# Reading the page numbers of the sample attention eight at a time into registers

## The chip, the cores and the metric

The kernel runs on one core of a Trainium2 chip. Five engines work side by side, each with a sequencer of its own that takes instructions in order: TensorE (PE in the profile, PEld for its weight loads), VectorE (DVE), ScalarE (ACT), GpSimd (POOL) and SyncE (SP, which only issues transfers and waits). They meet through semaphores. The metric is the device time of one execution in microseconds; lower is better.

## The reference, cut to what matters

One inference step of a two-layer decoder: layer 0 is multi-head latent attention, layer 1 an RWKV-7 time mix, each with a feed-forward block behind it. Beside a prompt of 528 tokens there are eight samples of four new tokens each. A sample attends to 4096 past positions, which lie in a paged cache: 32 pages of 128 positions, each page 256 latent columns and 64 rope columns. Which physical page holds which logical page is read from a table:

```
page_table   (DEC_BATCH, PAST_LEN // PAGE_SIZE) int32      logical page -> physical page
...
    s = jnp.einsum('bhtr,bsr->bhts', q_lat, c) + jnp.einsum('bhtp,bsp->bhts', q_rope, kr)
    s = s.astype(jnp.float32) * SOFTMAX_SCALE
    s = jnp.where(k_pos[None, :] <= q_pos[:, None], s, jnp.finfo(jnp.float32).min)
    p = jax.nn.softmax(s, axis=-1).astype(c.dtype)
    return jnp.einsum('bhts,bsr->bthr', p, c)
```

For a sample, `c` and `kr` are its 32 pages followed by its four new rows.

## The kernel before

The kernel is written engine by engine: a block holds one instruction stream for each engine, in a fixed order, and semaphores tie the streams together. The page table lies in SBUF as `ptab`, one row of 256 numbers.

**Where pages go.** There are two sets of page buffers, `u` = 0 and 1; sample b uses set b % 2. A set's 32 pages are in four groups of eight (`GP = 8`), with semaphores of their own: `page_full` and `ropes_full` say that a group has landed, `page_used` that PE has read it for the last time.

**Who issues the transfers.** `load_pages` is called by three engines, each for its part of the same groups. In the sample attention SP brings the latents of the pages whose number is not 3 modulo 4 (six of eight in a group), POOL the ropes of the same pages, and ACT both parts of the other two pages. For each page it loads one number from `ptab` into a register (line 564), checks that it lies in the pool, and issues one transfer (line 567, latent) or two (lines 567 and 571). Samples 0 and 1 are loaded by SP and POOL alone, during the prompt attention, with table positions known when the program is built. For samples 2 to 7 the loads stand in loops (`Fori`) over k, two samples to a turn.

**The sample attention.** PE turns the keys of four pages at a time (g = 0 to 7, and the new rows as g = 8) and scores them; ACT copies what PE turned out of PSUM (line 961 the rope part, line 965 the latents); PE mixes with the weights of the sample before in between (line 906), which sets that sample's pages free. So the copies of a sample are nine steps on ACT's stream. ACT's own page loads stand in this stream: behind the copies of steps 5, 6, 7 and 8 come the loads of groups 0, 1, 2 and 3 of the next sample that uses the freed set:

```
if g >= 5 and load is not None:
    load_pages(act, *load, [3], [3], [g - 5])
```

While six of the eight samples are copied, a set is refilled for a later sample; for the first and the last sample copied there is nothing to load beside the copies. ACT's stream also holds the exponents of the sample before (line 977), behind the copies of step 1.

Of the kernel before, what the change touches and what calls it, by code (L numbers as in the profile page):

```python
# [17 lines left out]
ALU = mybir.AluOpType  # L18
ACT = mybir.ActivationFunctionType
AX = mybir.AxisListType.X  # L20

P = 128
D = 1024
# [13 lines left out]
PAGE, PAGES = 128, 32  # L37
# [104 lines left out]
def program(nc, w, o):  # L142

    ctx = ExitStack()
    with ctx:
# [31 lines left out]
        ptab = sb("ptab", [1, DB * PAGES], I32)  # L177
# [108 lines left out]
        xtok, _ = carve(0, 5, D)  # L286
        vrow, _ = carve(5 * D, 2, P)
# [66 lines left out]
        at = 0  # L354
        q, at = carve(at, 3, H, T)
        q_end = at
        kT, at = carve(at, 3, T)
        ctok, at = carve(at, 5, KL + ROPE)
        after_keys = at
        z, at = carve(at, ZC, T)  # L360
        qn, at = carve(at, 2, T)
        ukT, at = carve(at, 2, KL)
        rt, at = carve(at, 2, T)
# [171 lines left out]
        even_lat, at = carve(after_keys, PAGES, KL)  # L535
        even_rope, at = carve(at, PAGES // 2, 2 * ROPE)
        cnew, at = carve(at, DB, KL + ROPE)
        LB = wb.all.shape[1] // KL
        RA = (PAGES - LB) * KL
        ropes = [wa.all[:, a:a + 2 * ROPE] for a in range(RA, wa.all.shape[1] - 2 * ROPE + 1, 2 * ROPE)][:PAGES // 2]  # L540
        while len(ropes) < PAGES // 2:
            more, at = carve(at, 2 * ROPE)
# [5 lines left out]
        GP = 8  # L548
# [3 lines left out]
        ptab_in, cnew_in = sem("ptab_in"), sem("cnew_in")  # L552
        n_pool = w["cache_latent"].shape[1]

        def load_pages(eng, k, u, latents=(), ropes=(), groups=range(PAGES // GP)):


            for g in groups:
                if not isinstance(k, int):
                    eng.wait_ge(page_used[u][g], k)  # L560
                for p in range(g * GP, (g + 1) * GP):
                    if p % 4 not in {*latents, *ropes}:
                        continue
                    page = eng.value_load(ptab[0:1, bass.ds(k * (2 * PAGES) + (u * PAGES + p), 1)], min_val=0,
                                          max_val=n_pool - 1)
                    if p % 4 in latents:
                        eng.dma_start(lat_of[u][p], w["cache_latent"][0, page]).then_inc(page_full[u][g], 16)
                    if p % 4 in ropes:

                        full = (page_full if p % 4 == 3 else ropes_full)[u][g]  # L570
                        eng.dma_start(rope_of[u][p // 2][:, p % 2 * ROPE:(p % 2 + 1) * ROPE],  # L571
                                      w["cache_krope"][0, page]).then_inc(full, 16)
# [139 lines left out]
        with nc.Block(no_gpsimd_drain=True) as block:  # L712
            @block.sync
            def _(sp):
                sp.dma_start(ptab[:], w["page_table"].rearrange("b n -> (b n)").rearrange("(a n) -> a n", a=1)).then_inc(ptab_in, 16)
                for b in range(DB):
                    sp.dma_start(cnew[0:DS, b], ctok[TAIL + b * DS:TAIL + (b + 1) * DS, 4]).then_inc(cnew_in, 16)
                sp.wait_ge(ptab_in, 16)
                load_pages(sp, 0, 0, range(4), [3])
                load_pages(sp, 0, 1, range(4), [3])  # L720

            @block.gpsimd
            def _(pool):
                pool.wait_ge(ptab_in, 16)
                load_pages(pool, 0, 0, ropes=range(3))
                load_pages(pool, 0, 1, ropes=range(3))

            @block.tensor
            def _(pe):
                scores(pe, 0, 0, 0)  # L730

                def step(i, u, g, gn, an):
                    if gn is not None:
                        scores(pe, i + 1, 1 - u, gn)
                    turn_and_mix(pe, i, u, g)
                over_tiles(pe, step)

            @block.scalar
            def _(act):
                exponents(act, 0, 0, 0)  # L740

                def step(i, u, g, gn, an):
                    if gn is not None:
                        keep_below(act, i + 1, 1 - u, gn)
                    keep_turned(act, i, u, g)
                    if gn is not None:
                        exponents(act, i + 1, 1 - u, gn)
                    keep_mixed(act, i, u, g)
                over_tiles(act, step)

            @block.vector
            def _(dve):
                stage(dve, 0, 0)
                stage(dve, 1, 1)
                mask_and_max(dve, 0, 0, 0, 0)
                weigh(dve, 0, 0, 0)

                def step(i, u, g, gn, an):
                    if not isinstance(i, int) or i + 2 < NT:
                        stage(dve, i + 2, u)  # L760
                    if gn is not None:
                        mask_and_max(dve, i + 1, 1 - u, gn, an)
                        weigh(dve, i + 1, 1 - u, gn)
                over_tiles(dve, step)
# [21 lines left out]
        kts, _ = carve(q_end, 2, 10, P)  # L786
        omix, _ = carve(q_end + 20 * P, RC, P)
        maxes, _ = carve(q_end + 22 * P, 4)
        sums, _ = carve(q_end + 22 * P + 4, 4)
        shift, _ = carve(q_end + 22 * P + 8, 1)  # L790
        of_q, _ = carve(q_end + 22 * P + 16, NQ)
        recip, _ = carve(q_end + 22 * P + 16 + NQ, NQ)
# [23 lines left out]
        with nc.Block(no_gpsimd_drain=True) as block:  # L816
            @block.sync
            def _(sp):
                with sp.Fori(1, DB // 2) as k:
                    for u in range(2):  # L820
                        load_pages(sp, k, u, range(3))

                for g in range(PAGES // GP):
                    sp.wait_ge(page_used[0][g], DB // 2)
                sp.dma_start(wuv, w["attn_w_uv"][0].rearrange("(c p) h n -> p c (h n)", p=P)).then_inc(wuv_in, 16)

            @block.gpsimd
            def _(pool):
                with pool.Fori(1, DB // 2) as k:
                    for u in range(2):  # L830
                        load_pages(pool, k, u, ropes=range(3))

            @block.tensor
            def _(pe):
# [116 lines left out]
            @block.scalar  # L951
            def _(act):
                def copies(b, before=None, load=None):

                    for g in range(NG + 1):
                        keys = turned_keys(g)
                        act.wait_ge(gscored, b * (NG + 1) + (g - 1 if 2 <= g < NG else 0) + FREE)
                        act.wait_ge(rope_turned, b * (NG + 1) + (g + 1))
                        r = slice(8, 10) if g < NG else slice(2, 3)
                        n = 2 if g < NG else 1  # L960
                        nc.scalar.copy(keys[:, r], ps[:, ROT, 0:n * P].rearrange("p (c n) -> p c n", n=P)).then_inc(rope_copied, 1)
                        for half in range(2 if g < NG else 1):
                            n = 4 if g < NG else 2
                            act.wait_ge(lat_turned, b * LATS + (g * 2 + half + 1))
                            nc.scalar.copy(keys[:, half * 4:half * 4 + n],
                                           ps[:, LAT[half], 0:n * P].rearrange("p (c n) -> p c n", n=P)).then_inc(lat_copied, 1)
                        if g == 1 and before is not None:
                            exponents(before)
                        if g >= 5 and load is not None:
                            load_pages(act, *load, [3], [3], [g - 5])  # L970

                def exponents(b):
                    act.wait_ge(shifted, b + 1 + FREE)
                    ge(act, p_turned, b * 2)
                    ge(act, sums_in, b)
                    for half in range(2):
                        nc.scalar.activation(probs_b[:, half * 4:half * 4 + 4], ps[:, SCORES + half].rearrange("p (g n) -> p g n", n=P),
                                             ACT.Exp, bias=shift, scale=SCALE, accum_out=sums[:, half:half + 1]).then_inc(exped_b, 1)
                    nc.scalar.activation(p_new[0:NQ], s_new[0:NQ], ACT.Exp, bias=shift[0:NQ], scale=SCALE,
                                         accum_out=sums[0:NQ, 2:3]).then_inc(exped_b, 1)  # L980

                copies(0)

                def step(k, u, b, last):
                    if last < 2:
                        copies(b + 1, b, None if last else (k + 1, u))
                    else:
                        exponents(b)
                over_batches(act, step)
# [1384 lines left out]
```

## Time and profile before

| what | value |
|---|---|
| three runs, lowest / median / highest | 2320.49 / 2325.57 / 2333.77 us |
| the profiled execution: its time | 2321.38 us |
| its span, first to last instruction | 2319.8 us |
| TensorE busy / weight loads busy | 2073.4 us (89%) / 1768.6 us (76%) |
| VectorE / ScalarE / GpSimd busy | 789.9 / 592.7 / 223.1 us |
| mean granted TensorE clock, 1 = full | 0.927 |

The span is what the trace covers; the time adds 1.6 us around it. Busy time is work on an engine's data path: register instructions, branches, semaphore waits and the issuing of transfers belong to the sequencer and are not in it. The sequencer's instructions have a q in the engine's name (ACTq) and can be looked up line by line.

### The profile page before, as it was taken

What the parts mean: (1) busy time and instruction counts of PE and PEld (TensorE: products, weight loads), DVE (VectorE), ACT (ScalarE), POOL (GpSimd) and SP (SyncE); (2) the same over time, 40 slices, a digit from 0 to 9 for tenths busy, and PEclk for the clock granted to TensorE, in tenths of its full rate; (3) what the DMA queues carried; (4) which work ended last, traced back from release to release, by engine and by line L of the source; (5) the groups of instructions that cost most, each with busy time, mean ns of one, the idle gap of its engine ahead of it and who ended that gap; (6) DMA issues with size and microseconds to landing.
All of it is one profiled execution on the core that took longest, in us unless ns stands there. A gap on an engine that the chain in (4) does not pass through costs nothing. (4 is left out here: it accounts for less than half of the span.)

```text
span 2319.8 us, 50416 instructions
## 1 busy us (share of the span) xinstructions
PE 2073.4 (89%) x20520; PEld 1768.6 (76%) x20520; DVE 789.9 (34%) x1283; ACT 592.7 (26%) x1023; POOL 223.1 (10%) x354
## 2 busy tenths in 40 slices
PE   4779889787895999999879999999988959999995
PEld 3546556566575999999847777888875759999995
DVE  3223432121204332233382342355553043322233
ACT  1112335343302322122212431222220033212222
POOL 0001300433200000000000320132220000000000
PEclk7888899887897999999989999999995979999998
DMA  3021400644322332332211320000002123242311
GB/s 108 13 59 49 135 26 2 177 140 139 110 73 55 91 99 69 87 90 75 65 37 55 90 65 10 4 13 8 12 12 57 37 75 88 82 118 64 104 57 50
DMA packets 270485, 156.56 MB, mean 67 GB/s; under 512 B 42504, under 2 KB 265455, under 8 KB 270192
## 3 DMA queue, kind: packets, MB, share of 16 engines
q1 hardware_dynamic: 250084, 139.99, 21.5%
q10 hardware_dynamic: 14092, 7.95, 1.2%
q0 software_dynamic: 6144, 6.30, 1.1%
q8 instruction: 119, 1.95, 0.4%
q14 instruction: 46, 0.38, 0.1%
HBM read 148.81 MB, written 5.34 MB: 66 GB/s over the span
## 5 line engine op out<-in xcount | busy, mean ns | idle before, releaser
L1125 PE MATMUL ps<-ffn_xh,ffn_wh 128*128 128x280 f32 (+1 forms) x1408 | 296.1, 292 | 27.8 <-DVE ffn_xl L1131 27.8
L1125 PE MATMUL ps<-ffn_xh,ffn_wl 128*128 128x280 f32 (+1 forms) x1408 | 293.7, 290 | 0.0
L1125 PE MATMUL ps<-ffn_xl,ffn_wh 128*128 128x280 f32 (+1 forms) x1408 | 293.6, 290 | 0.0
L1125 PEld LDWEIGHTS ps<-ffn_xh,ffn_wh 128*128 128x128 f32 x1408 | 224.1, 190 | 29.4 <-issue 29.4
L1125 PEld LDWEIGHTS ps<-ffn_xl,ffn_wh 128*128 128x128 f32 x1408 | 223.9, 190 | 0.0
L1125 PEld LDWEIGHTS ps<-ffn_xh,ffn_wl 128*128 128x128 f32 x1408 | 222.7, 190 | 0.0
L1131 DVE TENSOR_TENSOR ffn_wl<-wa,ffn_wh 128x1024 fp32r<-128x1024 f32 x88 | 107.7, 1225 | 219.2 <-ACT ffn_wh L1209 219.2
L1125 PE MATMUL ps<-ffn_hid_h,ffn_wh 128*128 128x280 f32 (+1 forms) x704 | 147.0, 290 | 0.0
L1125 PE MATMUL ps<-ffn_hid_h,ffn_wl 128*128 128x280 f32 (+1 forms) x704 | 146.3, 289 | 0.0
L1125 PE MATMUL ps<-ffn_hid_l,ffn_wh 128*128 128x280 f32 (+1 forms) x704 | 146.2, 289 | 0.0
L1209 ACT CAST ffn_wh<-wa 128x1024 fp32r<-128x1024 f32 x88 | 91.7, 1044 | 198.0 <-PE ps L1125 198.0
L1454 PE MATMUL ps<-arena,wa 128*128 128x280 f32 x512 | 124.8, 402 | 0.0
L1454 PEld LDWEIGHTS ps<-arena,wa 128*128 128x128 f32 x512 | 96.0, 190 | 28.3 <-issue 6.2
L1125 PEld LDWEIGHTS ps<-ffn_hid_h,ffn_wh 128*128 128x128 f32 x704 | 111.1, 188 | 0.0
L1125 PEld LDWEIGHTS ps<-ffn_hid_l,ffn_wh 128*128 128x128 f32 x704 | 111.1, 188 | 0.0
L1125 PEld LDWEIGHTS ps<-ffn_hid_h,ffn_wl 128*128 128x128 f32 x704 | 110.7, 189 | 0.0
L571 POOL DMA_DIRECT2D arena<-in_cache_krope x120 | 64.8, 540 | 448.9 <-issue 448.9
L1209 ACT CAST ffn_wh<-wb 128x1536 fp32r<-128x1536 f32 (+1 forms) x32 | 43.8, 1369 | 182.7 <-PE ps L1125 182.7
L1317 DVE TENSOR_TENSOR xT<-xT,ps 128x560 f32<-128x560 f32 (+1 forms) x32 | 23.3, 730 | 172.7 <-PE ps L1125 172.7
L1591 POOL TENSOR_TENSOR arena<-arena 128x560 f32<-128x560 f32 x8 | 9.4, 1176 | 713.4 <-ACT arena L1551 713.4
L615 PE MATMUL ps<-arena,hT 128*128 128x512 f32 (+8 forms) x204 | 75.8, 500 | 2.0 <-DVE hT L667 2.0
L1306 DVE TENSOR_TENSOR hT<-hT,ps 128x560 f32<-128x560 f32 (+1 forms) x44 | 32.1, 730 | 129.4 <-PE ps L1125 129.4
(331 smaller groups left out, 3427.0 us busy)
## 6 DMA issues: line engine op xcount, KB each, us to landing
wa<-in_ffn_w_gate SPq DMA_DIRECT2D x44, 512.0 KB, 3.9
wa<-in_ffn_w_up SPq DMA_DIRECT2D x44, 512.0 KB, 3.9
arena<-in_cache_latent SPq DMA_DIRECT2D x104, 128.0 KB, 2.2
wb<-in_ffn_w_down SPq DMA_DIRECT2D x16, 768.0 KB, 4.7
wb<-in_ffn_w_down SPq DMA_DIRECT2D x16, 640.0 KB, 4.2
wb<-in_cache_latent SPq DMA_DIRECT2D x73, 128.0 KB, 2.2
wa<-in_attn_w_o SPq DMA_DIRECT2D x8, 512.0 KB, 3.9
wa<-in_rwkv_w_r SPq DMA_DIRECT2D x8, 512.0 KB, 3.8
```

The source lines that it names most:

```text
L571: eng.dma_start(rope_of[u][p // 2][:, p % 2 * ROPE:(p % 2 + 1) * ROPE], w["cache_krope"][0, page]).then_inc(full, 16)
L615: mm = nc.tensor.matmul(ps[:, b, 0:n], qst[0:k, u, c], kT[0:k, c, a:a + n], start=c == 0, stop=c == 2)
L1125: mm = nc.tensor.matmul(dst[:, s, 0:n_half], a[:, c * P:(c + 1) * P], b[:, c, s * n_half:(s + 1) * n_half], start=first and n == 0, stop=l ...
L1131: return nc.vector.tensor_tensor(low, x, high.bitcast(F32), ALU.subtract)
L1209: nc.scalar.copy(wh[:, m_slot(m, slab), 0:chunks * P], ring.buf[s][:, 0:chunks * P]).then_inc(high, 1)
L1306: nc.vector.tensor_tensor(split(gate[:, u]), split(gate[:, u]), halves(4 * u + 2, half), ALU.mult).then_inc(risen, 1)
L1317: nc.vector.tensor_tensor(x, x, halves(2 * u, half), ALU.add).then_inc(added, 1)
L1454: mm = nc.tensor.matmul(ps[:, b + s, 0:HALF], wa.view(u, DC, P)[:, c], xmix[3 + t // DC][:, c, s * HALF:(s + 1) * HALF], start=c == 0, sto ...
L1591: nc.gpsimd.tensor_tensor(r[:, m], r[:, m], wfull[:, m % 2, 1:T + 1], ALU.mult).then_inc(r_scaled, 1)
```

## The change

`load_pages` loads the eight numbers of a group with one instruction into eight registers, once for each group and engine, and checks all eight before the first transfer of the group, also those whose pages another engine brings. The transfers stay the same, in the same order and on the same engines.

```diff
-        def load_pages(eng, k, u, latents=(), ropes=(), groups=range(PAGES // GP)):
+        def load_pages(eng, which, k, u, latents=(), ropes=(), groups=range(PAGES // GP)):
             for g in groups:
                 if not isinstance(k, int):
                     eng.wait_ge(page_used[u][g], k)
+                at = g * GP + u * PAGES
+                _, pages = nc.values_load_multi_w_load_instructions(
+                    ptab[0:1, at:at + GP] if isinstance(k, int) else ptab[0:1, bass.ds(k * (2 * PAGES) + at, GP)],
+                    engines=[which], min_val=0, max_val=n_pool - 1)
                 for p in range(g * GP, (g + 1) * GP):
-                    if p % 4 not in {*latents, *ropes}:
-                        continue
-                    page = eng.value_load(ptab[0:1, bass.ds(k * (2 * PAGES) + (u * PAGES + p), 1)], min_val=0,
-                                          max_val=n_pool - 1)
+                    page = pages[p - g * GP]
...
-                            load_pages(act, *load, [3], [3], [g - 5])
+                            load_pages(act, ACTE, *load, [3], [3], [g - 5])
```

ACT's stream before, behind the copies of step 5 in the first turn of the loop (`TENSOR_LOAD` reads the table; the two `ISA` rows behind it are the check, one for the comparisons and one for the assertion; an `ISA` row ahead of it or of a transfer works out an address):

```order
222 L560 REGISTER_ALU
223 L564 ISA
224 L564 TENSOR_LOAD ptab
225 L564 ISA x2
226 L567 ISA
227 L567 DMA arena<-in_cache_latent 128x256
228 L571 ISA
229 L571 DMA arena<-in_cache_krope 128x64
230 L564 ISA
231 L564 TENSOR_LOAD ptab
232 L564 ISA x2
233 L567 ISA
```

The same place of ACT's stream after the change (line 563 is the load, 569 and 573 the transfers):

```order
222 L561 REGISTER_ALU
223 L563 ISA
224 L563 TENSOR_LOAD ptab
225 L563 ISA x16
226 L569 ISA
227 L569 DMA arena<-in_cache_latent 128x256
228 L573 ISA
229 L573 DMA arena<-in_cache_krope 128x64
230 L569 ISA
231 L569 DMA arena<-in_cache_latent 128x256
232 L573 ISA
233 L573 DMA arena<-in_cache_krope 128x64
```

Two loads and two checks have become one load and eight checks, sixteen instructions, all ahead of the group's first transfer; ACT uses two of the eight numbers.

SP's stream before, at the head of its loop in the sample attention:

```order
336 L564 ISA
337 L564 TENSOR_LOAD ptab
338 L564 ISA x2
339 L567 ISA
340 L567 DMA arena<-in_cache_latent 128x256
341 L564 ISA
342 L564 TENSOR_LOAD ptab
343 L564 ISA x2
```

and after the change:

```order
224 L563 ISA
225 L563 TENSOR_LOAD ptab
226 L563 ISA x16
227 L569 ISA
228 L569 DMA arena<-in_cache_latent 128x256
229 L569 ISA
230 L569 DMA arena<-in_cache_latent 128x256
231 L569 ISA
```

Six loads with a check each have become one load with eight checks, and the six transfers follow one another with an address instruction between them. POOL's stream changes in the same way. PE's and DVE's streams are unchanged.

## Rows read from the trace of the kernel before

**Rows 1.** The page's first line.

```profile
span 2319.8 us, 50416 instructions
```

**Rows 2.** Busy time by stretch: us, engines, granted clock, DMA share, GB/s.

```profile
core 0: us, PE busy (x) PEld busy (x) DVE busy (x) ACT busy (x) POOL busy (x), PEclk, DMA share, GB/s
392.81:408.72 15.91, 14.53 (x225) 11.20 (x223) 4.60 (x17) 8.92 (x22) 1.35 (x3) 1.00 0.07 22
408.72:424.57 15.85, 11.09 (x146) 8.46 (x145) 2.99 (x9) 4.68 (x12) 6.96 (x14) 0.91 0.73 204
...
460.92:479.60 18.68, 16.90 (x217) 13.19 (x218) 3.89 (x14) 8.94 (x22) 4.01 (x8) 0.77 0.22 63
479.60:494.59 14.99, 11.12 (x146) 8.48 (x145) 2.98 (x9) 4.68 (x12) 6.64 (x13) 0.84 0.72 208
...
613.57:622.09 8.52, 8.14 (x139) 6.73 (x136) 2.16 (x7) 4.88 (x11) 0.00 (x0) 1.00 0.30 118
```

**Rows 3.** PE's waits from 395 to 620 us: total us, times, longest.

```profile
PE ps L844 <- ACT arena L961: 20.3, 15, 4.3
PE ps L874 <- ACT hT L965: 11.6, 6, 2.0
```

**Rows 4.** ACT's timeline in a step with loads: start, length, what, idle before.

```profile
413.98 0.37 ACT L961 COPY arena<-ps 128x256 f32<-128x256 f32 x1 [3.75 <-PE ps L881]
...
414.93 0.36 ACTq L567 DMA_DIRECT2D arena<-in_cache_latent  x1
...
416.57 0.35 ACTq L567 DMA_DIRECT2D arena<-in_cache_latent  x1
...
417.53 0.37 ACT L961 COPY arena<-ps 128x256 f32<-128x256 f32 x1 [2.20 <-PE ps L881]
```

**Rows 5.** ACT's timeline in the last sample, which loads nothing.

```profile
616.20 0.37 ACT L961 COPY arena<-ps 128x256 f32<-128x256 f32 x1 [1.17 <-PE ps L844]
...
618.23 0.37 ACT L961 COPY arena<-ps 128x256 f32<-128x256 f32 x1 [0.58 <-PE ps L844]
```

**Rows 6.** Line 564 on ACT in one step: ns min/median/max, first and last start.

```profile
L564 ACTq FUSED_REGOPS  x4: 51/102/152, 417.7 to 419.7; - x4
L564 ACTq TENSOR_LOAD <-ptab x2: 283/284/285, 417.8 to 419.4; - x2
L564 ACTq SEQ_ASSERT  x2: 18/18/18, 418.3 to 419.9; - x2
```

**Rows 7.** Lines 567 and 571 on ACT in the same step.

```profile
L567 ACTq FUSED_REGOPS  x2: 42/42/42, 418.4 to 420.0; - x2
L567 ACTq MOVE arena<-in_cache_latent x2: 29/29/29, 418.4 to 420.0; - x2
L567 ACTq DMA_DIRECT2D arena<-in_cache_latent x2: 349/349/349, 418.5 to 420.1; - x2
...
L571 ACTq FUSED_REGOPS  x2: 37/37/37, 418.9 to 420.5; - x2
...
L571 ACTq DMA_DIRECT2D arena<-in_cache_krope x2: 339/339/339, 419.0 to 420.6; - x2
```

**Rows 8.** Line 564 on ACT over the whole execution.

```profile
L564 ACTq TENSOR_LOAD <-ptab x48: 279/283/489, 409.8 to 595.1; - x48
```

**Rows 9.** SP: its last transfer of samples 0 and 1; two of its waits.

```profile
301.39 0.33 SPq L571 DMA_DIRECT2D arena<-in_cache_krope  x1
...
SPq L712 <- PEq L712: 71.0, 1, 71.0
...
SPq L564 <- PE ps L906: 62.5, 6, 31.6
```

**Rows 10.** POOL's last transfer into a set; its landing times; PE's first use of it.

```profile
434.31 0.53 POOL L571 DMA_DIRECT2D arena<-in_cache_krope  x1 [0.68 <-issue]
...
arena<-in_cache_krope POOLq DMA_DIRECT2D x120, 32.0 KB, 2.3
...
439.92 0.44 PE L844 MATMUL ps<-con,arena 128*128 128x128 f32 x2
```

More of the change, by code:

```diff
@@ L20 @@
 AX = mybir.AxisListType.X
+SPE, POOLE, ACTE = mybir.EngineType.SP, mybir.EngineType.Pool, mybir.EngineType.Activation
 P = 128
@@ L718, in _ @@
                 sp.wait_ge(ptab_in, 16)
-                load_pages(sp, 0, 0, range(4), [3])
-                load_pages(sp, 0, 1, range(4), [3])
+                load_pages(sp, SPE, 0, 0, range(4), [3])
+                load_pages(sp, SPE, 0, 1, range(4), [3])
             @block.gpsimd
@@ L724, in _ @@
                 pool.wait_ge(ptab_in, 16)
-                load_pages(pool, 0, 0, ropes=range(3))
-                load_pages(pool, 0, 1, ropes=range(3))
+                load_pages(pool, POOLE, 0, 0, ropes=range(3))
+                load_pages(pool, POOLE, 0, 1, ropes=range(3))
             @block.tensor
@@ L820, in _ @@
                     for u in range(2):
-                        load_pages(sp, k, u, range(3))
+                        load_pages(sp, SPE, k, u, range(3))
                 for g in range(PAGES // GP):
@@ L830, in _ @@
                     for u in range(2):
-                        load_pages(pool, k, u, ropes=range(3))
+                        load_pages(pool, POOLE, k, u, ropes=range(3))
             @block.tensor
```

## The prediction

> **What bounds the kernel now.** I read the page first: PE is busy most of the span [rows 1], so a change pays or costs only where PE waits. The change touches SP, POOL and ACT in two stretches: the prompt attention (loads of samples 0 and 1) and the sample attention. The busy time by stretch comes next [rows 2]. The first stretch shown holds the steps 0 to 4 of a sample: PE is busy 14.53 of 15.91 us, so PE is the bound. The next one, 408.72 to 424.57, holds the steps 5 to 8, in which ACT also issues page loads: PE is busy only 11.09 of 15.85 us, and ACT's data path 4.68. In the last sample, with the same steps and no loads, these steps take 8.52 us and PE is busy 8.14. So in the loading steps neither data path is the bound. The waits say who holds PE up [rows 3]: ACT's copies, 20.3 and 11.6 us, and no wait of PE in that view is put down to a transfer.
>
> ACT's timeline shows why [rows 4]. From the copy at 413.98 to the next step's copy at 417.53 are 3.55 us, and what lies between is the issuing of two pages: a latent and a rope from 414.93, the second latent and rope from 416.57. A page takes 416.57 - 414.93 = 1.64 us of ACT's sequencer, two take 3.28, and with the some 0.27 us of the copies' own issue that is the step. Without loads a step takes 618.23 - 616.20 = 2.03 us [rows 5]. So the bound of a loading step is ACT's sequencer, and whatever is added to its instructions there is added to the step, until it is less than what PE needs. There are 48 loads on ACT [rows 8], two in a step: 24 such steps.
>
> **The change on ACT, step by step.** One page costs, by the medians of one step [rows 6, 7]: address 51 ns, table load 283, comparison 152 (the largest of line 564's register instructions; the 51 is the address), assertion 18, then 42 + 29 + 349 for the latent and 37 + 29 + 339 for the rope (both MOVEs at 29). That is 1329 ns in ten instructions; the 1640 measured leave 31 ns between two of them.
>
> After the change a step has one address instruction, one load, eight comparisons with eight assertions, and the same four transfers: 51 + 283 + 8 x (152 + 18) + 2 x (42 + 29 + 349 + 37 + 29 + 339) = 334 + 1360 + 1650 = 3344 ns, and 30 instructions x 31 = 930 between them, together 4.27 us, and x for the seven further registers. Against 3.28 that is 0.99 us more and x. The load that is saved is cheaper than the six checks that are added, since ACT needs only two of the eight numbers.
>
> Two costs are not shown by any row. First, x. From below it is 0, if one read fills eight registers. From above it is seven further reads in full: a load is 283 ns, a MOVE 29, so the read is at most 254, and x at most 1.78 us. The only row is that of a load of one register, and it is nearly all waiting for the table: I take seven reads in turn, less an instruction's own handling and gap, 283 - 51 - 31 = 201 ns each, x = 1.41. The Trainium skill ("Runtime: NRT & Kernel Launch", Instruction fetch mechanics) says that a register load costs about 200 ns for each register even in bulk; no row here loads more than one, so the trace can't say yet. By that rule eight would take 1.6 us, x = 1.32, and the step 2.31 us more. The rule speaks against this change: a load of eight saves none of the reads.
>
> Second, whether the 152 ns belong to the comparison or are a wait for the loaded number. If they are a wait, the seven later comparisons cost about 51 each, like the address instruction, and the step is 7 x 0.101 = 0.71 us cheaper: 0.28 + x. I take 152: the load's duration differs (279 to 489 [rows 8]), and a wait for it should differ with it, but the step shows the 152 beside loads of 283 and 285 alike. At the end nearest to nothing, the step still gains nothing: 0.28 us more.
>
> So a loading step takes 0.99 + 1.41 = 2.40 us longer, 24 of them 57.6 us. Nothing covers it: PE's work in a step is at most the 2.03 us of a step without loads [rows 5], below the 3.55 now.
>
> **What comes behind it.** In the loading steps PE idles more, and its granted clock falls between the two levels of 2.4 and 1.2 GHz: 1.00 in the stretch 392.81 to 408.72, 0.91 in the loading steps behind it, 0.77 in 460.92 to 479.60 [rows 2]. The steps 0 to 4 took 15.91 us at 1.00 and 18.68 at 0.77, 2.77 us more. Six samples come behind loading steps, so at most 6 x 2.77 = 17 us could be added if none had it yet; some have it already, and I add 5, an estimate. Sum: 57.6 + 5 = 63 us.
>
> **SP and POOL.** In the sample attention each brings six of eight pages, so six loads and six checks become one load and eight checks. With ACT's durations for a transfer of one kind: before 6 x (51 + 283 + 152 + 18 + 42 + 29 + 349 + 7 x 31) = 6.85 us for a group, after 51 + 283 + 1360 + 6 x 420 + 36 x 31 + x = 5.33 + x, 6.74 with my x: nothing gained or lost, and 1.5 us gained with x = 0. It hides behind the attention: SP itself waits 62.5 us for PE's last use of pages [rows 9]. In the prompt attention the last transfer of samples 0 and 1 goes out at 301.39, and SP then waits 71.0 us for the block's end, at PE's pace, before anyone reads a page [rows 9]. The first transfer of a group goes out later than now by seven checks and x, 7 x (152 + 18 + 2 x 31) = 1.6 + 1.4 = 3.0 us. What would be late is a set's last group: its last rope is issued at 434.31 and lands some 2.3 us later, at 436.6, and PE takes the group up at 439.92 [rows 10], 3.3 us later. Since the four slower steps of ACT lie before that use, it moves back by 4 x 2.40 = 9.6 us, so the margin grows. If that cover went, a late group would cost about 3 us for each sample, 18 in all.
>
> **The rivals.**
> One read fills all eight registers, x = 0, with comparisons at 152: 24 x 0.99 = 24 us, and 2 of clock, 2347. For it: a burst of 32 bytes in one row. Against it: nothing measured.
> The 152 is a wait, and the reads are in turn: 24 x (0.28 + 1.41) = 41, and 3 of clock, 2365. Against it speaks the constancy of the 152.
> Both at once: 24 x 0.28 = 7 us, 2328, which is no change to be told from noise.
> Faster: PE's waits of 20.3 us at the turning of ropes [rows 3] would in truth be pages that land late, put down to ACT's semaphore because ACT's copy came last; the SP and POOL loads, 1.5 us shorter for a group at x = 0, would bring them in time. It decides if pages land after PE could take them; then it gives at most 20.3 - 7 = 13 us, 2308. Rows 10 speak against it, and so does the last sample [rows 5], whose pages are brought in the same way and whose steps run at 2.03.
> Clock: PE, idle for longer in each loading step, is granted the lower level through the steps 0 to 4 too. These 14.53 us of busy PE [rows 2] would take up to twice as long, 6 x 14.5 = 87 us, 2466 with the 58. Against it: the grants come back within the stretch in every sample now.
>
> **How the numbers follow.** The sum is made against the profiled execution's 2321.4 us, which lies 4 below the median of the three runs, 2325.6, and inside their range. 2321.4 + 63 = 2384. Chances: forecast 0.48, one read 0.22, short comparisons 0.14, both 0.08, faster 0.03, clock 0.05. The range of 2340 to 2415 holds the first three: its lower end lies under 2347 by the runs' spread, its upper end takes x = 1.78, 24 x 2.77 = 66, and 17 of clock, 2405, and the same spread. It leaves out 0.16. About 0.5% (12 us) is what a measurement of this kernel can tell from no change: faster 0.03, the same 0.08, slower 0.48 + 0.22 + 0.14 + 0.05 = 0.89.
>
> **What would show it.** On ACT, the load's new duration gives x directly: about 283 ns for one read, 1.5 to 1.7 us for reads in turn. The eight comparisons show whether the later ones are 152 or 51. The distance of the copies at the steps 5 to 8 should grow from 3.55 to about 5.95 us, and the step distance in the last sample stay at 2.03. PE's waits for ACT's copies should grow by about 58 us and no wait for a transfer appear. It would be wrong if the steps grow by less than ACT's instructions do, so that something covers them, or if the steps 0 to 4 change by more than the 5 us of clock.

## The result and the profile after

| what | before | after |
|---|---|---|
| median of the runs timed on one chip | 2329.43 us (4 runs) | 2354.61 us (4 runs, 2353.15 to 2361.71) |
| ratio, with its 95% interval | | 1.0119 [1.0079, 1.0159] |
| the profiled execution | 2321.38 us | 2354.87 us |
| mean granted TensorE clock | 0.927 | 0.918 |

The change makes the kernel 1.2% slower, some 28 us by the ratio. The forecast was 2384 us with a range of 2340 to 2415: the direction and the range hold, the likeliest value is 29 us too high. Counted as a change, the forecast was 63 us, and some 28 were measured.

The page's first line after the change, against [rows 1]:

```profile
span 2353.2 us, 50304 instructions
```

There are 112 fewer instructions, and the span is 33.4 us longer; this pair of executions differs by some 6 us more than the ratio says. Line numbers shift by a few from kernel to kernel: 961 before, 963 after and 964 or 968 further down are the same copy. Busy time by stretch after the change, the same five stretches as in [rows 2]; the first sum below is that of the loading steps (5 to 8) of all six samples that load, the second that of the steps 0 to 4 of samples 1 to 7:

```profile
core 0: us, PE busy (x) PEld busy (x) DVE busy (x) ACT busy (x) POOL busy (x), PEclk, DMA share, GB/s
391.77:407.68 15.91, 14.53 (x225) 11.20 (x223) 4.60 (x17) 8.93 (x21) 0.53 (x1) 1.00 0.01 4
407.68:428.35 20.67, 13.96 (x149) 10.05 (x147) 3.08 (x9) 4.69 (x12) 11.72 (x23) 0.69 0.76 227
470.71:489.85 19.14, 17.36 (x217) 13.47 (x218) 3.90 (x14) 8.96 (x22) 0.49 (x1) 0.75 0.01 2
489.85:509.88 20.03, 13.68 (x149) 9.93 (x147) 2.99 (x9) 4.69 (x12) 9.72 (x19) 0.69 0.76 224
646.36:654.88 8.52, 8.14 (x139) 6.73 (x136) 2.16 (x7) 4.88 (x11) 0.00 (x0) 1.00 0.31 121
...
sum 129.26, PE 81.26 PEld 59.96 DVE 18.26 ACT 28.12 POOL 66.60; mean PE 13.54 PEld 9.99 DVE 3.04 ACT 4.69 POOL 11.10
...
sum 125.33, PE 113.14 PEld 87.57 DVE 27.43 ACT 62.41 POOL 10.90; mean PE 16.16 PEld 12.51 DVE 3.92 ACT 8.92 POOL 1.56
```

The same two sums of the kernel before:

```profile
sum 100.18, PE 68.05 PEld 51.66 DVE 18.14 ACT 28.11 POOL 43.75; mean PE 11.34 PEld 8.61 DVE 3.02 ACT 4.69 POOL 7.29
...
sum 120.58, PE 109.62 PEld 85.28 DVE 27.44 ACT 62.48 POOL 33.24; mean PE 15.66 PEld 12.18 DVE 3.92 ACT 8.93 POOL 4.75
```

In this pair of traces the two kinds of stretch hold the loss: 129.26 - 100.18 = 29.1 us in the loading steps and 125.33 - 120.58 = 4.8 us in the steps 0 to 4, together 33.8 against the 33.4 of the span. The last sample, which loads nothing, takes the same 8.52 us as before. In the first and the third of the six loading stretches the granted clock fell from 0.91 and 0.84 to 0.69, and PE's busy time grew with it (11.09 to 13.96 us in the first), while PE still idles about a third of the stretch.

ACT's timeline in a loading step after the change, against [rows 4]:

```profile
418.52 0.37 ACT L963 COPY arena<-ps 128x256 f32<-128x256 f32 x1 [3.41 <-PE ps L883]
418.79 1.08 ACT L967 COPY arena<-ps 128x512 f32<-128x512 f32 x2
421.30 0.34 ACTq L569 DMA_DIRECT2D arena<-in_cache_latent  x1
421.80 0.34 ACTq L573 DMA_DIRECT2D arena<-in_cache_krope  x1
422.30 0.34 ACTq L569 DMA_DIRECT2D arena<-in_cache_latent  x1
422.79 0.34 ACTq L573 DMA_DIRECT2D arena<-in_cache_krope  x1
423.25 0.27 ACT L963 COPY hT<-ps 128x128 f32<-128x128 f32 x1 [3.37 <-issue]
```

The step from copy to copy is 423.25 - 418.52 = 4.73 us, where it was 3.55. The four transfers now follow each other at 0.50 us, and the first of them goes out 2.78 us behind the copy. What stands ahead of it is line 563, here by its instructions in this step (ns min/median/max, first and last start):

```profile
L563 ACTq FUSED_REGOPS  x9: 51/147/152, 418.7 to 420.9; - x9
L563 ACTq SEQ_ASSERT  x8: 18/18/18, 419.6 to 421.1; - x8
L563 ACTq TENSOR_LOAD <-ptab x1: 541/541/541, 418.8 to 418.8; - x1
```

The load of eight numbers takes 541 ns. One number took 283 [rows 6, 8], so a further one costs (541 - 283) / 7 = 37 ns on average. The eight comparisons take 147 to 152 ns each, where the one of before took 152. With their assertions and the gaps between them the eight checks come to some 1.8 us, the greater part of the 2.78 (an experiment below takes them out).

PE's waits from 395 to 660 us after the change, against [rows 3] (total us, times, longest):

```profile
PE ps L846 <- ACT arena L963: 33.4, 18, 4.8
PE ps L876 <- ACT hT L967: 16.2, 6, 3.1
```

The two waits for ACT's copies grew from 20.3 to 33.4 and from 11.6 to 16.2 us, together by 17.7. No wait for a transfer appeared. That is less than the 29.1 us by which the loading steps grew, since PE's own work took longer at the lower granted clock: its busy time there went from 68.05 to 81.26 us.

The steps of the last sample, against [rows 5], are 2.03 us as before:

```profile
648.99 0.37 ACT L963 COPY arena<-ps 128x256 f32<-128x256 f32 x1 [1.17 <-PE ps L846]
...
651.02 0.37 ACT L963 COPY arena<-ps 128x256 f32<-128x256 f32 x1 [0.58 <-PE ps L846]
```

And SP's wait for PE's last use of pages, against the 62.5 us of [rows 9]: SP has more time left than before, not less.

```profile
SPq L563 <- PE ps L908: 105.5, 6, 30.2
```

### The profile page after: what moved, and what is told of

The parts are those of the page before. It is cut to its first block and busy times, and to the rows that moved or that the text cites. A ratio compares the mean times of both kernels' runs of the same rounds, so it can differ in the third digit from the quotient of the medians.

```text
span 2353.2 us, 50304 instructions
## 1 busy us (share of the span) xinstructions
PE 2090.6 (89%) x20520; PEld 1778.8 (76%) x20520; DVE 789.9 (34%) x1283; ACT 592.9 (25%) x1023; POOL 223.6 (10%) x354
```

## Experiments

The theory: a loading step is as long as ACT's instructions in it, and what the change costs is six bounds checks too many, less one load, plus 37 ns for each further number that is loaded. The rivals are that SP's and POOL's later transfers cost the time, that it is the eight-wide load itself, and that something other than ACT's stream sets the steps.

**Which engine's edit costs the time.** Two kernels divide the change. In the first only ACT reads eight at a time, and SP and POOL read as before; the second is its opposite (`single = which is ACTE`):

```diff
+                single = which is not ACTE
...
+                    page = eng.value_load(ptab[0:1, bass.ds(k * (2 * PAGES) + (u * PAGES + p), 1)], min_val=0,
+                                          max_val=n_pool - 1) if single else pages[p - g * GP]
```

> ACT alone loads eight numbers at once; SP and POOL load one beside each transfer, as before. If the loss is the instructions on ACT's sequencer in the 24 loading steps, the step stays at 4.7 us as in the changed kernel and the time is 1.2% above before, 29 us. If SP's and POOL's later or denser transfers cost the time, the kernel comes out within 0.3% of before.

> SP and POOL load eight numbers at once; ACT loads one beside each transfer, as before. ACT theory: the loading step is back at 3.55 us and the time within 0.3% of before, although a group's first transfer goes out some 2 us later. Theory of SP and POOL: up to 1.2% above before, with waits of PE for pages.

The edit on ACT alone took 2352.29 us, 1.0127 [1.011, 1.0145] of the kernel before; that on SP and POOL alone 2324.75 us, 1.0011 [0.9997, 1.0024]. A step of ACT in the first:

```profile
424.48 0.37 ACT L968 COPY arena<-ps 128x256 f32<-128x256 f32 x1 [3.40 <-issue]
...
429.22 0.27 ACT L968 COPY hT<-ps 128x128 f32<-128x128 f32 x1 [3.39 <-issue]
```

and in the second:

```profile
422.89 0.37 ACT L968 COPY arena<-ps 128x256 f32<-128x256 f32 x1 [2.24 <-PE ps L888]
...
426.43 0.27 ACT L968 COPY hT<-ps 128x128 f32<-128x128 f32 x1 [2.19 <-issue]
```

4.74 us against 3.54: the loss is ACT's. The rival that SP's and POOL's later transfers cost it falls: the interval leaves them at most 0.24%.

**What of ACT's line costs it.** The changed kernel without the bounds checks on ACT (SP and POOL keep theirs):

```diff
-                    engines=[which], min_val=0, max_val=n_pool - 1)
+                    engines=[which], min_val=0, max_val=n_pool - 1,
+                    skip_runtime_bounds_check_because="page_table holds pool pages" if which is ACTE else None)
```

> The changed kernel without the bounds checks on ACT (they are left out there; SP and POOL keep theirs; the outputs are the same). If the eight comparisons and assertions are the loss, 8 x (147 + 18 + 58) ns = 1.8 us leave the step: 4.74 becomes 2.95 us, below the 3.55 of before, and the time is 24 x 0.6 = 14 us or 0.6% below before. If the load of eight registers is the loss, the step stays above 3.55 and the time above before.

It took 2290.0 us, 0.9854 [0.9836, 0.9872], faster than both kernels. Its steps, still with a load of eight (545 to 548 ns):

```profile
415.62 0.37 ACT L964 COPY arena<-ps 128x256 f32<-128x256 f32 x1 [1.61 <-PE ps L884]
...
418.55 0.27 ACT L964 COPY hT<-ps 128x128 f32<-128x128 f32 x1 [1.57 <-PE ps L884]
```

2.93 us, 1.80 less than with eight checks: a check costs 1.80 / 8 = 0.23 us of ACT's sequencer. But the gain against before is 34 us by the ratio, 28.2 between the two profiled executions, and 24 x (3.55 - 2.93) = 15, which was expected, does not explain it. The stretches give the rest of the 28.2: the loading steps took 77.30 us in all instead of 100.18, 8 us more than those 15, and the steps 0 to 4 took 115.13 instead of 120.58. Most of the 8 us lies at the two turns of ACT's loop, which the experiments on that turn, below, take up.

The second kernel on this question reads, on ACT, only the two numbers that it needs, with one load of every fourth number, and checks those two:

```diff
+                if which is ACTE:
+                    quads = ptab.rearrange("o (n f) -> o n f", f=4)
+                    src = quads[0:1, bass.ds(k * (2 * PAGES // 4) + at // 4, 2), 3]
...
+                    page = pages[(p - g * GP) // 4 if which is ACTE else p - g * GP]
```

> The changed kernel, but ACT loads just the two numbers that it uses, with one load of two registers and two checks. By the load's durations for one and eight registers (283 and 541 ns, 37 ns for each further one) this load takes 320 ns and the step 4.74 - 6 x 0.224 - 6 x 0.037 = 3.18 us, 0.37 less than before: 9 us or 0.4% below before. If a load of several registers had a fixed price of its own (some 540 ns whatever the number), the step would be 3.4 us and the time within 0.2% of before.

2309.79 us, 0.9947 [0.993, 0.9964]. The load and a step:

```profile
L568 ACTq TENSOR_LOAD <-ptab x24: 479/482/680, 406.4 to 571.6; - x24
```

```profile
414.35 0.37 ACT L968 COPY arena<-ps 128x256 f32<-128x256 f32 x1 [2.08 <-PE ps L888]
...
417.70 0.27 ACT L968 COPY hT<-ps 128x128 f32<-128x128 f32 x1 [2.00 <-issue]
```

The step is 3.35 us, 0.20 below before. The load was expected at 320 ns and the step at 3.18 us; both came out longer. Two numbers that lie 16 bytes apart take 482 ns, and 482 - 283 = 199 for the second: nearly as long as all eight neighbours together (541). Either the price of a further number depends on where it lies, or a load of several has a fixed price of its own whatever their number; the next kernel tells these apart.

**Eight numbers that are not neighbours.** The changed kernel once more, with the same instructions on every engine, but ACT's load of eight reads every fourth number (a window that ends on the two it needs):

```diff
+                    src = quads[0:1, bass.ds(k * (2 * PAGES // 4) + (at // 4 - 6), 8), 3]
...
+                    page = pages[6 + (p - g * GP) // 4 if which is ACTE else p - g * GP]
```

> The changed kernel with the same instructions on ACT, but its load of eight registers reads every fourth number of the table instead of eight neighbours (it uses the last two, which are its pages). One strided load of eight took 1728 ns where it was hidden, eight neighbours take 541. If the forecast failed in the price of the load alone, the step is now 4.74 + 1.19 = 5.93 us, the forecast's 5.95, and the time 24 x 1.19 = 28 us above the changed kernel, 2383, 2.4% above before. If something covers part of a longer step, it stays nearer to the changed kernel's 1.2%.

The changed kernel ran again on the same chip:

> The changed kernel again, on the chip of the strided one: 1.2% above before, the step of ACT at 4.74 us, the load of eight neighbours at 541 ns.

2383.55 us, 1.0243 [1.0199, 1.0288], against 2356.77 us, 1.0124 [1.0081, 1.0167], for the changed kernel. The load, and two of its steps:

```profile
L568 ACTq TENSOR_LOAD <-ptab x24: 1716/1734/1932, 409.7 to 651.9; - x24
```

```profile
415.69 0.37 ACT L968 COPY arena<-ps 128x256 f32<-128x256 f32 x1 [5.57 <-issue]
...
421.67 0.37 ACT L968 COPY arena<-ps 128x256 f32<-128x256 f32 x1 [4.63 <-issue]
...
427.71 0.27 ACT L968 COPY hT<-ps 128x128 f32<-128x128 f32 x1 [4.69 <-issue]
```

Here each of the seven further numbers costs (1734 - 283) / 7 = 207 ns, so no fixed price for a load of several explains the rows: the price of a further number follows its place. x is 1.45 us and the step 5.98 to 6.04 us, where the forecast had 201 ns, 1.41 and 5.95, met by a kernel that differs from the changed one in nothing but the place of the numbers in the table. So the forecast's chain from a load to a step holds, and the place decides the one price that failed. That the time too is the forecast's 2384 is partly chance: the kernel lies 58 us above the median of before on its chip, and the forecast added 63 to an execution below that median.

**The turn of ACT's loop.** In the kernel of two numbers ACT passes from one turn of its loop to the next much faster than before. The last copy of one turn and the first copy of the next, in the kernel before:

```profile
452.59 0.27 ACT L961 COPY hT<-ps 128x128 f32<-128x128 f32 x1 [2.21 <-issue]
...
460.92 0.37 ACT L961 COPY arena<-ps 128x256 f32<-128x256 f32 x1 [7.79 <-issue]
```

and in the kernel of two numbers:

```profile
448.64 0.27 ACT L968 COPY hT<-ps 128x128 f32<-128x128 f32 x1 [2.02 <-issue]
...
452.32 0.37 ACT L968 COPY arena<-ps 128x256 f32<-128x256 f32 x1 [3.14 <-issue]
```

8.33 us became 3.68. Between the branch at the loop's end and the next instruction ACT stands still for 4.36 and 3.33 us at the two turns before, and for 0.23 us here. A turn of ACT's loop executes 287 instructions before, 367 after the change, 271 here (counted in the traces). To see whether the length does it, the same kernel was given 16 instructions a sample that only raise a semaphore nobody waits for, placed where ACT has time, at step 4:

```diff
+                        if g == 4 and load is not None:
+                            for _ in range(16):
+                                act.sem_inc(passed)
```

> The kernel with loads of two registers on ACT, with 16 semaphore instructions that nobody waits for added to ACT's stream behind the copies of step 4, where ACT waits for PE. They cost some 16 x 0.06 = 1 us a sample there, hidden. If the stall at the loop's turn comes from the length of ACT's loop body (287 executed instructions with the stall, 271 without), it is back at 3.3 to 4.4 us, twice, and the time 7 to 10 us above that of the unpadded kernel, 0.2% below before or nothing. If the stall has another cause, the turns stay at 0.23 us and the time 0.5% below before.

2323.42 us, 0.9984 [0.9967, 1.0]: the gain of the two-number load is gone. The same two copies:

```profile
455.50 0.27 ACT L968 COPY hT<-ps 128x128 f32<-128x128 f32 x1 [2.03 <-issue]
...
463.43 0.37 ACT L968 COPY arena<-ps 128x256 f32<-128x256 f32 x1 [7.38 <-issue]
```

7.93 us, and behind the branch 4.1 and 3.25 us of standing still, with 303 instructions in a turn. The added instructions themselves cost nothing that shows: the padded kernel's steps 0 to 4 take 15.81 us in the second sample. On ACT the gap behind the branch is 0.23 us in every kernel here whose turn has 126, 239, 258 or 271 instructions and 2.54 to 4.43 us where it has 287, 303 or 367. That explains most of the 8 us of the kernel without checks (239 instructions): 4.36 + 3.33 - 2 x 0.23 = 7.2. The Trainium skill ("Runtime: NRT & Kernel Launch", Instruction fetch mechanics) says that a taken branch whose target lies outside the window of two instruction pages makes the engine fetch the page first, a page being 256 instructions. The rule is one of pages and not of a length, and the other engines' loops speak against a length alone. SP's loop turned at once with 339 instructions in the kernel before:

```profile
L819 SPq COMPARE_BRANCH  x1: 58/58/58, 464.9 to 464.9; - x1
L819 SPq MOVE  x1: 34/34/34, 465.2 to 465.2; - x1
```

and stood still for 3.0 us with 291 after the change:

```profile
L821 SPq COMPARE_BRANCH  x1: 53/53/53, 466.1 to 466.1; - x1
L821 SPq MOVE  x1: 43/43/43, 469.2 to 469.2; - x1
```

POOL's loop did the same (0.21 to 0.25 us with 339, 3.45 to 4.13 with 291); there it costs nothing, since both then wait for PE's last use of pages. So 271 and 287 are figures of ACT's loop in its place in the program. That the standing still is the fetching of a page, and where the borders of the pages lie, no run here shows.

**Out of ACT's critical steps.** The numbers of all four groups of a sample are known when its loads begin. So ACT reads its eight numbers of a sample with one load behind the copies of step 4, checks them there, and the steps 5 to 8 only issue transfers:

```diff
+                    page = held[p // 4] if which is ACTE else pages[p - g * GP]
...
+                        if g == 4 and load is not None:
+                            quads = ptab.rearrange("o (n f) -> o n f", f=4)
+                            _, held = nc.values_load_multi_w_load_instructions(
+                                quads[0:1, bass.ds(load[0] * (2 * PAGES // 4) + load[1] * (PAGES // 4), PAGES // 4), 3],
+                                engines=[ACTE], min_val=0, max_val=n_pool - 1)
                         if g >= 5 and load is not None:
-                            load_pages(act, ACTE, *load, [3], [3], [g - 5])
+                            load_pages(act, ACTE, *load, [3], [3], [g - 5], held)
```

> ACT reads the eight numbers that it needs for a whole sample with one load and eight checks behind the copies of step 4, where it waits for PE for over 4 us, and the steps 5 to 8 hold the transfers alone. If a loading step is the sum of ACT's instructions, it falls to 2.93 - 0.55 - 0.08 = 2.3 us, and the load and its checks, 2.4 us, are hidden behind PE's mixing: 24 x (3.55 - 2.3) = 30 us below before; 8 more since the loop body on ACT is short enough to turn without the stall of 3.3 to 4.4 us, and some 7 of clock: 1.9% below before. If pages become late now that a sample takes 25 us, PE waits for transfers and the gain is under 1%.

2283.17 us, 0.9823 [0.9785, 0.9862]. A sample in two stretches, steps 0 to 4 and then the loading steps with the passage to the next sample:

```profile
446.14:461.95 15.81, 14.06 (x218) 10.65 (x218) 3.96 (x15) 8.83 (x22) 6.42 (x12) 1.00 0.48 144
461.95:472.04 10.09, 9.37 (x146) 7.55 (x145) 2.55 (x7) 4.68 (x11) 5.65 (x11) 1.00 0.83 248
```

The load takes 1.73 us and the eight checks some 1.8 more, and the steps 0 to 4 still take 15.81 us: PE's work covers them. The loading steps took 63.58 us in all instead of 100.18, PE is busy 9.37 of 10.09 us in the stretch shown, and its granted clock stays at 1.00. Of the 36.6 us that they gain, 4.36 + 3.33 - 2 x 0.23 = 7.2 are the turns of ACT's loop, which has 258 instructions here and turns in 0.23 us; the numbers' place in the stream is not the only thing that changed. PE now also waits for transfers, 2.2 us in all. This is the fastest version here that keeps every check on the numbers it uses.

**All page loads off ACT.** ACT loads no page at all, and SP brings the other two latents and ropes too, first with the checks and then without those of SP and POOL:

```diff
-                        load_pages(sp, SPE, k, u, range(3))
+                        load_pages(sp, SPE, k, u, range(4), [3])
...
-                        if g >= 5 and load is not None:
-                            load_pages(act, ACTE, *load, [3], [3], [g - 5])
```

> No page loads on ACT: SP brings all latents and the ropes of every fourth page, POOL the other ropes, with eight numbers at once and eight checks. ACT theory: the steps 5 to 8 fall to 2.03 us, and SP becomes the bound: a group costs it 0.7 + 8 x 0.26 + 10 x 0.52 = 7.9 us, a sample 31.5, against 34 now: 0.5 to 1% below before, with waits of PE that are for pages. If SP's work hides whatever it is, a sample takes 23 us and the time is 2.8% below before.

> The same without bounds checks on SP and POOL (left out; the outputs are the same). A group costs SP 0.7 + 10 x 0.52 = 5.9 us, a sample 23.5, just what the steps of a sample take when none loads (23): 66 us or 2.8% below before. If checks are cheap on SP, it equals the checked kernel.

With checks 2315.78 us, 0.9959 [0.9938, 0.998]; without them 2266.87 us, 0.9753 [0.9723, 0.9782]. With checks, PE waits for pages at the turning of the ropes (from 395 to 620 us):

```profile
PE ps L846 <- DMA arena<-in_cache_krope: 14.5, 6, 4.7
PE ps L846 <- DMA wa<-in_cache_krope: 11.7, 5, 3.5
```

SP's stream shows why; these are its first transfers of one group and of the next:

```profile
429.87 1.89 SPq L569 DMA_DIRECT2D arena<-in_cache_latent  x4
...
438.32 1.98 SPq L569 DMA_DIRECT2D wb<-in_cache_latent  x3
```

8.45 us for a group, 33.8 for the four groups of a sample, where PE could take a sample in 24.6 us (below). From 395 to 640 us SP waits for PE's last use of pages only once, so its sequencer becomes the bound as ACT's was. POOL takes some 6.0 us for a group. Without checks a sample takes 15.91 + 8.66 = 24.57 us:

```profile
416.60:432.51 15.91, 14.53 (x225) 11.20 (x223) 4.68 (x17) 8.93 (x22) 6.46 (x13) 1.00 0.66 193
432.51:441.17 8.66, 8.66 (x144) 7.32 (x143) 2.37 (x7) 4.93 (x12) 6.45 (x13) 1.00 0.72 216
```

PE is busy through the loading steps, at the full clock. This is what a sample takes here when no sequencer holds it up.

## Why the prediction was right, and where its size was off

**The bound.** Right. A loading step is as long as ACT's instructions in it: it followed them up (4.73 us after, 6.0 with the strided load) and down (3.35 with two numbers, 2.93 without checks), down to PE's own pace. "Nothing covers it" held too.

**The checks.** Right. The forecast's 152 ns for each comparison, taken as its own duration and not as a wait for the loaded number, are 147 to 152 in all eight; the rival of short comparisons (2365) falls by the row of line 563. The reason that the prediction gave was weaker than its result: loads of 283 and 285 ns hardly differ, so a comparison of 152 beside both did not rule a wait out. Were the other seven 51 ns, the step would have grown by 0.5 us and not by 1.18.

**x, the seven further registers.** Mis-sized, and the one term of the sum that the runs show to have failed: "I take seven reads in turn, less an instruction's own handling and gap, 283 - 51 - 31 = 201 ns each, x = 1.41". It measured 541 - 283 = 0.26 us. With it the step grows by 0.99 + 0.26 = 1.25 us by the forecast's own sum, and by 4.73 - 3.55 = 1.18 by the trace; 24 steps give 30 by the sum and 29.1 by the stretches, where the forecast had 57.6. The error has a reason that the prediction could have priced: it knew both bounds, 0 and 1.78, noted for the low one that the numbers are "a burst of 32 bytes in one row", and then placed x by the duration of a load of one number, which says nothing on how the next one is fetched. The rival of one read (2347, with x = 0) came out nearer the measured time. The Trainium skill ("Runtime: NRT & Kernel Launch", Instruction fetch mechanics) has about 200 ns for each register even in bulk; the runs agree with that, for a table in SBUF, where the numbers lie 16 bytes apart (199 and 207 ns), and not for eight neighbours (37 ns).

**The clock.** Its size is not settled by the runs. 5 us were added, and in the traces above the steps 0 to 4 took 4.8 more. But in the second profiled execution of the changed kernel they took 2.0 more than before:

```profile
sum 122.62, PE 110.47 PEld 85.40 DVE 27.42 ACT 62.26 POOL 10.57; mean PE 15.78 PEld 12.20 DVE 3.92 ACT 8.89 POOL 1.51
```

and 122.66 us in the kernel with SP's and POOL's edit alone, whose steps on ACT are those of before. So two executions differ by as much as the term itself, and that the estimate met one of them is luck. The loading steps do not scatter so: 129.26 and 129.90 us in the two executions of the changed kernel, 100.18 and 100.62 in the kernel before and the one with SP's and POOL's edit. The rival of a clock that stays low (2466) did not come: in the last sample the grant is 1.00, and in the steps 0 to 4 from 470.71 of the changed kernel it is 0.75, where it was 0.77 in the same steps before.

**SP and POOL.** Right that nothing is gained or lost in time: the edit there alone measures 1.0011 [0.9997, 1.0024], and no wait of PE for a transfer appears in the changed kernel.

**The faster rival**, pages that land late, falls with the same rows: it needed PE's 20.3 us of waits to be transfers', and they grew with ACT's step.

**What to look for.** "PE's waits for ACT's copies should grow by about 58 us" was wrong in kind as well as in size: of the 29.1 us only 17.7 are waits, because PE's granted clock fell in these steps, and its busy time, 13.2 us longer, fills part of them.

What stays open: how the sequencer fetches neighbouring numbers (by one access, or by several in a row) was not tried with other distances than 4 and 16 bytes, nor with fewer than eight neighbours, so the 37 ns are an average over seven.

## What to carry to other kernels

When an engine issues dynamic transfers between its own compute instructions, count its sequencer's time per step first; here it bounded steps in which every data path idled, and taking the reads and checks out of them (one load of the sample's numbers where PE's work covers it) gave 1.8%, some 0.3 of it by a faster turn of ACT's loop, where reading more at once in the same place lost 1.2%. A load of eight registers was cheap only for neighbouring numbers, and each number read brought its own check, 0.23 us against the 37 ns of a further neighbour: read few, and only those that the engine uses. Where a price isn't in the trace and its bounds are far apart, a row of the same operation at another size doesn't place it; give the end that the layout speaks for its full chance.

## What the runs showed of the hardware

- In the changed kernel a load of eight neighbouring 32-bit numbers takes 549 ns on ACT in the median (541 in the step shown), 527 on SP and 574 on POOL; on ACT one number takes 283 in the kernel before, two at a distance of 16 bytes 482, eight at that distance 1734.
- A runtime bounds check costs 0.23 us of ACT's sequencer, of which 147 to 152 ns are the comparison; the address instructions of the same kind in the steps shown take 37 to 51 ns.
- ACT's loop stands still for 2.54 to 4.43 us behind its branch when a turn has 287 or more instructions, and 0.23 us up to 271. SP's and POOL's loops turn within 0.25 us with 339 instructions and stand still for over 2.4 us with 291, so the length alone does not decide. Sixteen added instructions a sample cost about 0.4% on ACT in this way and through the clock behind it: 0.78 in the steps 0 to 4 from 463.43, 1.00 in the same steps without them.
- With the numbers read at step 4, the loading steps are 100.18 - 63.58 = 36.6 us shorter than before, and the profiled execution 2321.38 - 2277.66 = 43.7 us. PE's granted clock in the steps 0 to 4 behind them is higher: 1.00 in that version's stretch from 446.14, 0.77 in the same steps of the kernel before [rows 2], 0.75 after the change (0.89 in that kernel's second profiled execution).
